# First 256 inner columns of two feed forward parts made token tile by token tile in a two-block float32 kernel

## The reference

```
for i in range(2):
    mix = moba_attention(h, ...) if i == 0 else dilated_attention(h, ...)
    h = layer_norm(ALPHA * h + mix, ln_mix_g[i], ln_mix_b[i])
    h = layer_norm(ALPHA * h + square(relu(h @ w_in[i])) @ w_out[i], ln_mlp_g[i], ln_mlp_b[i])
```

## Time and profile before

| | |
|---|---|
| median of 3 runs | 1331.51 us |
| lowest and highest run | 1331.49 and 1333.16 us |
| profiled execution: span from first to last instruction | 1330.9 us |
| TensorE busy | 1177.8 us (88%) |
| VectorE busy | 690.8 us (52%) |
| ScalarE busy | 491.5 us (37%) |
| mean granted TensorE clock | 0.961 |

### The profile page before, as it was taken

How to read it: one execution, slowest core, us unless ns; L and a number is a source line. 1 busy time by engine, 2 the same in 40 slices (tenths; PEclk the granted TensorE clock), 3 DMA queues, 4 the chain that set the end, 5 groups by cost and what they waited for, 6 DMA issues and landing times.

```text
span 1330.9 us, 22159 instructions
## 1 busy us (share of the span) xinstructions
PE 1177.8 (88%) x9403; PEld 920.4 (69%) x9403; DVE 690.8 (52%) x1029; ACT 491.5 (37%) x711; POOL 3.9 (0%) x8
## 2 busy tenths in 40 slices
PE   6999999998885667657676899999999999999997
PEld 5688888886552334334243799888888899888886
DVE  4699867774220102011110677576666767766665
ACT  5653446553110100000000464554444456544442
POOL 0000000000000000000000000000000000000000
PEclk9999999999998888888788999999999999999999
DMA  9867587679999999999999964344636245463610
GB/s 356 304 216 262 179 308 269 253 322 407 426 424 426 428 428 425 427 428 429 429 426 420 302 236 175 143 158 159 248 132 243 91 160 199 149 249 131 249 68 32
DMA packets 92743, 369.94 MB, mean 278 GB/s; under 512 B 6654, under 2 KB 14636, under 8 KB 79604
## 3 DMA queue, kind: packets, MB, share of 16 engines
q1 hardware_dynamic: 92280, 367.92, 70.7%
q10 hardware_dynamic: 380, 0.81, 0.2%
HBM read 367.66 MB, written 1.05 MB: 277 GB/s over the span
## 4 chain that ended last, share of the span: by engine, by line
PE 72%; DMA 22%; DVE 2%; ACT 2%; issue 1%; SPq 1%; DVEq 0%; ACTq 0%
DMA arena<-in_moe_w 20%; PE ring L2189 8%; PE ring L2664 6%; PE ring L2178 5%; PE acc L2291 5%; PE acc L2292 5%; PE acc L2293 5%; PE ring L2191 4%; PE ring L2180 3%; DMA own<-in_moe_w 2%; PE acc L2162 2%; PE acc L2163 2%; PE acc L2164 2%; PE ring L2339 1%; PE ring L2341 1%; PE ring L2340 1%
## 5 line engine op out<-in xcount | busy, mean ns | idle before, releaser
L2664 PE MATMUL ring<-arena 128*32 128x256 f32 x1952 | 148.0, 468 | 73.6 <-DMA arena<-in_moe_w 72.4
L2664 PEld LDWEIGHTS ring<-arena 128*32 128x32 f32 x1952 | 75.4, 134 | 141.9 <-issue 74.8
L1409 DVE TENSOR_TENSOR wlo<-arena,whi 128x2048 fp32r<-128x2048 f32 x56 | 128.0, 2290 | 49.8 <-ACT whi L940 49.8
L1859 DVE TENSOR_TENSOR arena<-arena,ring 128x128 f32<-128x128 f32 x32 | 12.1, 379 | 255.2 <-ACT arena L1213 255.2
L1213 ACT ACTIVATE arena<-ring 128x128 f32<-128x128 f32 x32 | 8.9, 278 | 346.1 <-PE ring L2664 342.6
L940 ACT ACTIVATE whi<-arena 128x2048 fp32r<-128x2048 f32 x56 | 106.8, 1910 | 41.6 <-PE acc L2293 25.4
L2189 PE MATMUL ring<-xboth,whi 128*128 128x512 f32 x320 | 113.8, 398 | 0.0
L2191 PE MATMUL ring<-xboth,wlo 128*128 128x256 f32 x320 | 89.8, 281 | 0.0
L2189 PEld LDWEIGHTS ring<-xboth,whi 128*128 128x128 f32 x320 | 60.1, 188 | 14.8
L2178 PE MATMUL ring<-hboth,w1hi 128*128 128x512 f32 x192 | 68.0, 399 | 0.1
L2702 PE MATMUL acc<-above 32*128 32x256 f32 x512 | 46.0, 425 | 24.3 <-DVE above L1866 16.6
(11 more groups left out here) (448 smaller groups left out, 2685.6 us busy)
## 6 DMA issues: line engine op xcount, KB each, us to landing
arena<-in_moe_w SPq DMA_DIRECT2D x75, 2048.0 KB, 21.8
arena<-in_mlp_w_in SPq DMA_DIRECT2D x16, 2048.0 KB, 9.8
arena<-in_mlp_w_out SPq DMA_DIRECT2D x16, 2048.0 KB, 8.1
own<-in_moe_w SPq DMA_DIRECT2D x14, 2048.0 KB, 25.7
arena<-in_w_in SPq DMA_DIRECT2D x9, 2048.0 KB, 9.5
arena<-in_w_mod SPq DMA_DIRECT2D x6, 2048.0 KB, 13.1
arena<-in_moe_w SPq DMA_DIRECT2D x11, 1024.0 KB, 12.9
own<-in_w_mod SPq DMA_DIRECT2D x4, 2048.0 KB, 10.4
```

Of the source, the lines that this page charges most:

```text
L1409: dve.tensor_tensor(lo, raw, hi.bitcast(F32), ALU.subtract).then_inc(G["split_ready"], 1)
L2664: ins = pe.matmul(o, xs[:, kt, j, :], w[kt][g], start=(kt == 0), stop=(kt == KT - 1), skip_group_check=bool(early))
```

## The change

Chunk 0 of both feed forward parts is made with token columns stationary and 256 weight columns moving, tile by tile: `first_high` and `first_low` write `first_hidden(tt)`, 256 columns of `acc`. The products of tile 0 stand between the turns of tile 0 and those of tile 1 in TensorE's order. VectorE makes relu (one operation) and the square (another) for each tile into `hsq`; TensorE turns the four 128x128 pieces into the banks `(0, 0)` and `(0, 1)` (`first_turned`), ScalarE copies the high parts from there and VectorE subtracts for the low parts. Chunk 1 is made by `second_half`, for each bank eight high products and then eight low ones; its first bank stands ahead of the turns and its second behind them, and `bank_plan` has the order (1, 0), (0, 0), (0, 1), (1, 1). Before `hidden_out(0)` TensorE waits with `moved(pe, f"ff{l}", (0, 1))`.

The idle products of `KEPT` are gone in both places. The weight splits are moved: the first one ahead of the normalisation on both engines, the second between the tiles on ScalarE and behind `x_low` on VectorE, the third behind `x_high` on ScalarE and behind the squares on VectorE. The fourth (`hf + 3`) keeps its place between chunk 0's last step and chunk 1's first on both engines. `x_low(n, 0)` is moved ahead of the last step of the normalisation on VectorE, `x_high` 0 and 1 ahead of tile 1's root on ScalarE. The split buffers are taken in falling order. Two semaphores are added.

```diff
@@ -184,7 +184,8 @@
         order += [("xT", (2 * l + 1, i), "V") for i in range(4)]
-        order += [(f"ff{l}", (i, j), "V") for i in range(FF // 256) for j in range(2)]
+        order += [(f"ff{l}", at, "V") for at in ((1, 0), (0, 0), (0, 1), (1, 1))]
+        order += [(f"ff{l}", (i, j), "V") for i in range(2, FF // 256) for j in range(2)]
         if l == 0:
...
@@ -239,11 +240,11 @@
     elif _name[:3] == "ff_":
-        _buf = "w", (_h - HALF_AT[f"ff_in{_name[-1]}", 0, 0] + (2, 0)[int(_name[-1])]) % FB
+        _buf = "w", ((2, 1)[int(_name[-1])] - (_h - HALF_AT[f"ff_in{_name[-1]}", 0, 0])) % FB
     elif (_name, _s, _u) == ("proj1", 1, 0):
...
     else:
-        _buf = "w", (_h - HALF_AT[f"qkv{_name[-1]}", 0, 0] + 1) % WB
+        _buf = "w", (_h - HALF_AT[f"qkv{_name[-1]}", 0, 0] + (1, 0)[int(_name[-1])]) % WB
     BUF_OF.append(_buf[1])
...
@@ -449,7 +450,7 @@
         ROUTER_BLOCKS = 3
-        KEPT = {1: (0,), 2: (2,), 3: (2,), 4: (2,)}
+        KEPT = {1: (0,), 2: (), 3: (2,), 4: ()}
         ring = ctx.enter_context(nc.psum_tensor("ring", [P, RB, 512], F32))
...
@@ -595,6 +596,18 @@
             return acc[:, 1, 512 * tt:512 * tt + 512]
+        def later_chunk(l, i):
+            return (NFF - 1) * l + i - 1
+        def hidden_before(l, i):
+            return l * (2 * NFF - 1) + max(0, 2 * i - 1)
+        def first_hidden(tt):
+            return acc[:, 0, 512 * tt:512 * tt + 256]
...
@@ -1347,19 +1360,27 @@
                 hf = HALF_AT[f"ff_in{l}", 0, 0]
+                split_hi(hf)
                 square_roots()
-                split_hi(hf)
-                for tt in range(TT):
-                    layer_std(2 * l + 1, tt)
-                for i in range(4):
+                layer_std(2 * l + 1, 0)
+                split_hi(hf + 1)
+                for i in range(2):
                     x_high(2 * l + 1, i)
-                for i in range(1, FB):
-                    split_hi(hf + i)
-                for i in range(NFF):
-                    c = NFF * l + i
+                layer_std(2 * l + 1, 1)
+                for i in range(2, 4):
+                    x_high(2 * l + 1, i)
+                split_hi(hf + 2)
+                for j in range(2):
+                    ins = act.activation(hidhi[:, 0, j, :], take(f"ff{l}", (0, j))[:, 0:T], ACT.Copy)
+                ins.then_inc(G["hid_ready"], 1)
+                split_hi(hf + 3)
+                for i in range(1, NFF):
+                    c = later_chunk(l, i)
                     for j in range(2):
                         b = take(f"ff{l}", (i, j))
-                        if c >= 2 and j == 0:
+                        if j == 0 and c and i < 3:
+                            act.wait_ge(G["hsq_ready"], c)
+                        elif j == 0 and c:
                             act.wait_ge(G["hsq_ready"], c - 1)
...
@@ -1367,7 +1388,7 @@
                     for j in (2 * i + 2, 2 * i + 3):
-                        if FB <= j < 2 * NFF:
+                        if j < 2 * NFF:
                             split_hi(hf + j)
...
@@ -1947,9 +1968,11 @@
                 scaled(1)
+                if n % 2:
+                    x_low(n, 0)
                 shifted(1)
                 if n < 4:
-                    for i in range(4):
+                    for i in range(n % 2, 4):
                         x_low(n, i)
...
@@ -2085,24 +2108,34 @@
                 hf = HALF_AT[f"ff_in{l}", 0, 0]
+                split_lo(hf)
                 layer_norm(2 * l + 1, ln_mix, (ln_in[0], 32 * (l + 1)))
-                for i in range(FB):
-                    split_lo(hf + i)
-                for i in range(NFF):
-                    c = NFF * l + i
+                split_lo(hf + 1)
+                for tt in range(TT):
+                    b, r = first_hidden(tt), hsum[:, 0, tt, :]
+                    dve.wait_ge(G["first_product"], TT * l + tt + 1)
+                    link(dve.tensor_scalar(r, b, 0.0, None, ALU.max))
+                    dve.tensor_tensor(hsq[:, 0, tt, :], r, r, ALU.mult).then_inc(G["first_squared"], 1)
+                split_lo(hf + 2)
+                dve.wait_ge(G["hid_ready"], hidden_before(l, 0) + 1)
+                for j in range(2):
+                    b = take(f"ff{l}", (0, j))[:, 0:T]
+                    dve.tensor_tensor(hidlo[:, 0, j, :], b, hidhi[:, 0, j, :].bitcast(F32), ALU.subtract).then_inc(freed["V"], 1)
+                split_lo(hf + 3)
+                for i in range(1, NFF):
+                    c = later_chunk(l, i)
                     s, v = hsum[:, i % 2, :, :], hsq[:, i % 2, :, :]
...
                     moved(dve, f"ff{l}", (i, 1))
-                    if c >= 2:
-                        dve.wait_ge(G["hid_ready"], 2 * c - 2)
+                    dve.wait_ge(G["hid_ready"], hidden_before(l, i - 2) + 2 if i > 2 else hidden_before(l, 0))
                     dve.scalar_tensor_tensor(v, s, 0.0, s, ALU.max, ALU.mult).then_inc(G["hsq_ready"], 1)
-                    dve.wait_ge(G["hid_ready"], 2 * c + 1)
+                    dve.wait_ge(G["hid_ready"], hidden_before(l, i) + 1)
                     dve.tensor_tensor(hidlo[:, i % HB, :, :], v, hidhi[:, i % HB, :, :].bitcast(F32), ALU.subtract).then_inc(G["hid_ready"], 1)
                     for j in (2 * i + 2, 2 * i + 3):
-                        if FB <= j < 2 * NFF:
+                        if j < 2 * NFF:
                             split_lo(hf + j)
...
@@ -2190,6 +2223,19 @@
                     full(ins)
+            def second_half(b, h, j):
+                _, wh, wl = half_of(h)
+                m = slice(j * P, (j + 1) * P)
+                pe.wait_ge(G["whi_ready"], h + 1)
+                for kt in range(KT):
+                    pe.matmul(b.rearrange("p (s t) -> p s t", s=2), wh[:, kt, m], xboth[:, :, kt, :], start=(kt == 0), stop=False,
+                              skip_group_check=True)
+                pe.wait_ge(G["split_ready"], h + 1)
+                for kt in range(KT):
+                    ins = pe.matmul(b[:, T:2 * T], wl[:, kt, m], xhi[:, kt, :], start=False, stop=(kt == KT - 1), skip_group_check=True)
+                full(ins)
...
@@ -2302,9 +2348,9 @@
-            def turned_tokens(n, src, name="xT"):
-                for i in range(4):
+            def turned_tokens(n, src, name="xT", tiles=(0, 1)):
+                for i in range(2 * tiles[0], 2 * tiles[-1] + 2):
                     tt, q = divmod(i, 2)
...
@@ -2924,29 +2970,64 @@
                     proj_last(2)
-                turned_tokens(2 * l + 2, hres)
+                n = 2 * l + 1
+                def first_high(tt, q):
+                    _, wh, wl = half_of(HALF_AT[f"ff_in{l}", 0, 0])
+                    pe.wait_ge(G["xhi_ready"], highs_until(n, 2 * tt + q))
+                    t_ = slice(tt * P, (tt + 1) * P)
+                    for kt in range(4 * q, 4 * q + 4):
+                        for w in (wh, wl):
+                            pe.matmul(first_hidden(tt), xhi[:, kt, t_], w[:, kt, :], start=(kt == 0 and w is wh), stop=False,
+                                      skip_group_check=True)
+                def first_low(tt, q):
+                    _, wh, _ = half_of(HALF_AT[f"ff_in{l}", 0, 0])
+                    moved(pe, "xT", (n, 2 * tt + q))
+                    t_ = slice(tt * P, (tt + 1) * P)
+                    for kt in range(4 * q, 4 * q + 4):
+                        ins = pe.matmul(first_hidden(tt), xlo[:, kt, t_], wh[:, kt, :], start=False, stop=(kt == KT - 1), skip_group_check=True)
+                    if q:
+                        ins.then_inc(G["first_product"], 1)
+                def first_turned(j):
+                    b = bank(f"ff{l}", (0, j))
+                    for tt in range(TT):
+                        pe.wait_ge(G["first_squared"], TT * l + tt + 1)
+                        ins = pe.transpose(b[:, tt * P:(tt + 1) * P], hsq[:, 0, tt, j * P:(j + 1) * P], ident)
+                    full(ins)
...
                     h = HALF_AT[f"ff_in{l}", i // 2, i % 2]
+                    pair_half([bank(f"ff{l}", (i, j)) for j in range(2)], h)
+                turned_tokens(n + 1, hres, tiles=(0,))
+                pe.wait_ge(G["split_ready"], HALF_AT[f"ff_in{l}", 0, 0] + 1)
+                first_high(0, 0)
+                first_high(0, 1)
+                first_low(0, 0)
+                turned_tokens(n + 1, hres, tiles=(1,))
+                first_high(1, 0)
+                first_low(0, 1)
+                first_high(1, 1)
+                first_low(1, 0)
+                first_low(1, 1)
+                def hidden_out(i, tiles=(0, 1)):
                     if i == 0:
-                        banks = []
-                        def bank_part(j, low):
-                            if j == len(banks):
-                                banks.append(bank(f"ff{l}", (0, j)))
-                            return banks[j][:, 0:T] if low else banks[j][:, T:2 * T], True
-                        first_half(bank_part, h, 2 * l + 1, lambda j, ins: full(ins))
```

(16 more changed lines are left out.)

## The result

| | before | after |
|---|---|---|
| median | 1332.2 us (12 runs) | 1334.12 us (12 runs) |
| lowest and highest run | 1331.26 and 1334.24 us | 1331.75 and 1336.65 us |
| profiled execution, span | 1330.9 us | 1334.8 us |
| mean granted TensorE clock | 0.961 | 0.956 |

The ratio is 1.0016 with a 95% interval from 1.0008 to 1.0023: 1.9 us slower. The interval leaves out 1, so the loss is real, but it is less than the 0.2% that the prediction set as the bound of "same", and the interval reaches over that bound. The forecast was 1336.2 us, with a range of 1331.6 to 1338.6. The runs after are spread over 4.9 us, those before over 3.0. The median before is now 1332.2 us, 0.7 above that of the three runs that the prediction started from.

A forecast was written before the change was run, and what follows sets the result against it. The prediction took TensorE as the bound, with each layer's entry, up to the start of `hidden_out(0)`, left to move. It summed 1331.5 + 1.5 for the wait + 3.2 for two clock falls = 1336.2 us, range 1331.6 to 1338.6.

The forecast's parts named there:

- The products cost the same: TensorE's entry: 28 products behind `x_high(2)` take 3.47 us, chunk 1 5.62 us plus 0.44 for new turns; product cost unchanged.
- The entry's delays: Each layer's entry: the last normalisation step of tile 1 (L1941) starts 0.84 us late in layer 0, 0.53 in layer 1.
- The count that waits for chunk 1: Before out 0: the count of three comes only after split `hf + 3` and L2097, stalling TensorE 2.4 us per layer.
- rival D: Out 0 starts when TensorE gets there, without the wait: 3.3 us won, 1328.2 us; chance 0.12.
- The sum without the clock: Both layers' entries: out 0 later by 0.95 and 0.52 us, together 1.5 us slower.
- One fall of the clock in each layer: Behind each stall before out 0: TensorE's clock halves for 3.2 us, costing 1.6 us per layer, 3.2 us in all.
- B: Wait before out 0 and no fall of the clock: 1333.0 us; chance 0.22.
- C: Wait before out 0 and one fall of the clock: 1334.6 us; chance 0.17.
- A: Wait before out 0 and two falls of the clock: 1336.2 us; chance 0.38.
- The Trainium skill's rule: TensorE is throttled by default unless active; the removed idle products and the stalls before out 0 speak for two falls.

The follow-up runs named there:

- The filled wait: Changed kernel with two idle products of 512 columns ahead of the wait for out 0 in each layer: 1333.01 us, ratio 1.0006 to the kernel before.
- the second profile: Profile from running the changed kernel again with no edit: 1334.42 us, ratio 1.0018 to the kernel before.
- the right count: Changed kernel, out 0 waiting only for bank (0, 0), a count of two, with three waited for ahead of chunk 2: 1328.23 us, ratio 0.997.
- low part late: The kernel with the right count, but `x_low(n, 0)` back behind the normalisation's last step: 1332.42 us, ratio 1.0002 to the kernel before.
- without idle products: Kernel before the change, without the idle products ahead of tile 1's turns in both feed forward parts: 1333.96 us, ratio 1.0013.
- two splits: Changed kernel with the splits of half `hf + 4` moved up behind those of `hf + 3`: 1342.2 us, ratio 1.0077 to the kernel before.
- the root first: The kernel with the right count, but tile 1's root ahead of `x_high` 1 on ScalarE: 1329.73 us, ratio 0.9982 to the kernel before.

## Why the prediction was right, point by point

- **The products cost the same.** Right. The 28 products behind `x_high(2)` took 867.94 to 871.39, 3.45 us against 3.47. Chunk 1 with its turns took 871.39 to 877.57, 6.18 us to the end of the last product, where 6.06 from start to start was set.
- **The entry's delays.** Right in kind, too large in layer 0. L1938 (the old L1917) started 4.76 us ahead of tile 0's turns instead of 5.24, so the split made it 0.48 late where 0.64 was set, and L1962 (the old L1941) started 3.47 us behind them instead of 2.98, 0.49 late where 0.84 was set. VectorE made up 0.31 of its lateness by the first L1957 (1.35 us behind the turns against 1.18), where 0.22 was set. No run takes the moved split back alone, so its share is read from the rows.
- **The count that waits for chunk 1.** Right, and shown by three runs. From the end of the turns (874.18 + 0.60) to out 0 it was 4.99 us, 5.05 was set; the hole was 2.20 us, 2.4 was set. Undone in two different ways, the loss turns into 3.8 to 4.2 us of gain, where rival D had 3.3 for such a kernel. With a second split in the way the hole is 4.72 us.
- **The sum without the clock**, 1.5 us, was too large: it was 1.06 us, because of the entry's delays in layer 0. In layer 1 0.50 us was measured for 0.52.
- **One fall of the clock in each layer, 3.2 us.** This is the term that was mis-sized. Where a fall comes behind the hole it costs 1.6 us in layer 0 and 1.8 or 1.9 in layer 1 (1.6 was set). But it does not come in every execution: both profiles of the changed kernel have it in layer 1, one of them in layer 0, and the medians leave 0.9 to 1.3 us for both layers together. The prediction chose between two rows of before, one with a fall and one without, and for its time went by the first in both layers. That is why the median lies at 1334.1 and not at 1336.2, between the cases B and C. The runs reach from below B (1331.75) to A (1336.65), and the profiled execution, with both falls and 1336.56 us, was case A.
- **Where luck helped.** The forecast change was 4.7 us and the measured one 1.9. The time was missed by only 2.1 us because the median before came out 0.7 higher than that of the first three runs. And the range of 7 us takes in A, B and C together, so that the median lies in it says little about how often the clock falls; that the wait is what costs is shown by the runs and not by the time.
- **The Trainium skill's rule.** The Trainium skill ("TensorE: Matmul & The Clock Gate", Part 1) calls the throttled state the default and activity what releases it. The filled wait agrees: same schedule, clock 1.00 in both layers and 1.4 us less. Taken as a fall at both stalls of every execution it would have given 3.2 us; the runs gave 0.9 to 1.3, and layer 0 of the second profile kept 1.00 behind an unfilled hole.

What stays open is when a hole of 2.2 us brings the clock down and when not. The traces show that it did in three of the four holes of this length that were profiled in the changed kernel, and the medians leave room for less than one such fall in a run. Whether the other runs had fewer falls or shorter ones is not shown, and no run here was made to tell what decides it.

## What to carry to other kernels

When a semaphore counts releases and the waiting side derives its number from a planned order, the number is only right if the releasing engine works in that order; where the two differ, it names another event than the one that is needed. A later one, as ahead of out 0 here, is safe, but everything between the two events in that engine's queue is on the path. An earlier one, as for bank (1, 0) here, is not safe by itself, and another wait has to cover it. Look up the row that lets the waiting instruction go, and ask whether it is the one whose data it needs: here the right count changed 1.9 us of loss into 3.8 us of gain. A hole that cannot be closed can still be filled, which was worth 1.4 us here.

## What the runs showed of the hardware

A hole of 2.2 us between dense stretches of TensorE sufficed in some executions to halve its clock for a stretch of out products (2.80 us at 0.54, 3.00 at 0.50), and in the same kernel another hole of the same length, in the same place, left it at 1.00. Two idle products in the hole kept the clock up in both layers of the one profile.

The holes that were profiled, by length: of two of 1.95 and 1.96 us one brought a fall (low part late), of four of 2.2 us three (the changed kernel, twice), of two of 2.84 us both, the second a shorter one (without idle products), of two of 4.72 us both (two splits). Behind 4.72 us the half rate once cost 1.7 us, no more than behind 2.2, and once 2.7, when it lasted through 5.70 us.

The spread of a kernel's runs is a weak sign of such holes. It was 4.9 and 4.1 us in the changed kernel against 3.0 and 2.0 in the kernel before beside it, but 4.4 in the one with the root first, whose longest wait of TensorE in the entry is 0.86 us: its highest run, 1332.87 us, is the profiled one, and there the clock was at 0.50 from 733 to 737 us, in the expert stage, where the profile of before has 1.00.
